# In the heavy experts of a mixture-of-experts block, the four gate tiles of a slice are computed before its four up tiles

## The reference, cut to what matters

```
def moe_swiglu(h, w_router, w_gate, w_up, w_down):
    logits = jnp.einsum('bsd,de->bse', h, w_router).astype(jnp.float32)
    top_v, top_i = lax.top_k(logits, TOP_K)
    wts = jax.nn.softmax(top_v, axis=-1)
    gates = jnp.sum(jax.nn.one_hot(top_i, N_EXPERTS, dtype=jnp.float32) * wts[..., None], axis=-2)

    def per_seq(args):
        hb, gb = args
        a = jnp.einsum('sd,edf->sef', hb, w_gate)
        u = jnp.einsum('sd,edf->sef', hb, w_up)
        act = jax.nn.silu(a) * u * gb[:, :, None]
        return jnp.einsum('sef,efd->sd', act, w_down)
```

## Time and profile before

| | us |
|---|---|
| median of three launches | 2583.78 |
| the three launches | 2572.14, 2583.78, 2585.42 |
| the profiled launch, its own time | 2578.32 |
| its span, from the first to the last instruction | 2576.3 |
| TensorE busy in the span | 2470.6 (96%) |
| VectorE, ScalarE busy | 652.9, 375.5 |
| experts, from the first heavy rise to the last residual matmul | 703.4 to 1698.6 |

### The profile page before, as it was taken

The page is one execution under the profiler, slowest core; times in us unless marked ns, Lnnn a source line. Parts: engine busy times, 40 slices in busy tenths (PEclk is TensorE's granted clock), DMA queues, the critical chain, the costliest instruction groups (busy, mean ns, idle before and its releaser), DMA issues.

```text
span 2576.3 us, 34065 instructions
## 1 busy us (share of the span) xinstructions
PE 2470.6 (96%) x14632; PEld 1945.3 (76%) x14633; DVE 652.9 (25%) x1854; ACT 375.5 (15%) x973; POOL 28.0 (1%) x52
## 2 busy tenths in 40 slices
PE   7999999998999989998999899989899999989999
PEld 4768888876888558855885687567578888658888
DVE  3663452167200001000000000024531112443111
ACT  3231000223200000000000000014420001441001
POOL 1010000001000000000000000000000000000000
PEclk9999999997999999999999999999999999999999
DMA  9381777422277999799979988992334442423420
GB/s 359 130 293 67 288 267 261 143 99 99 99 261 294 368 394 339 277 395 394 349 278 394 394 336 298 394 308 95 131 107 155 153 139 69 145 100 131 154 75 17
DMA packets 270058, 582.85 MB, mean 226 GB/s; under 512 B 19386, under 2 KB 46530, under 8 KB 269908
## 3 DMA queue, kind: packets, MB, share of 16 engines
q1 hardware_dynamic: 268900, 579.51, 61.5%
q10 hardware_dynamic: 432, 1.01, 0.1%
q0 software_dynamic: 576, 0.13, 0.0%
HBM read 579.58 MB, written 1.05 MB: 225 GB/s over the span
## 4 chain that ended last, share of the span: by engine, by line
PE 87%; DMA 6%; DVE 3%; ACT 2%; issue 1%; SPq 0%; DVEq 0%; ACTq 0%
PE wrk L2204 16%; PE acc L1582 12%; PE acc L835 9%; PE wrk L2890 9%; PE acc L2240 7%; PE wrk L1565 6%; PE wrk L2217 5%; DMA ring<-in_moe_w_up_dram 5%; PE acc L838 3%; PE acc L909 2%; PE acc L2251 2%; PE acc L924 2%; PE acc L739 1%; PE acc L2259 1%; PE acc L2267 1%; PE wrk L974 1%
## 5 line engine op out<-in xcount | busy, mean ns | idle before, releaser
L2204 PEld LDWEIGHTS wrk<-hT,ring 128*128 128x128 f32 x3584 | 408.5, 194 | 26.1 <-issue 14.9
L2204 PE MATMUL wrk<-hT,ring 128*128 128x128 f32 x3584 | 411.3, 277 | 16.0 <-DMA ring<-in_moe_w_up_dram 9.3
L1582 PE MATMUL acc<-scratch,ring 128*128 128x256 f32 x1376 | 300.4, 379 | 0.0
L1582 PEld LDWEIGHTS acc<-scratch,ring 128*128 128x128 f32 x1376 | 261.1, 190 | 35.3
L835 PE MATMUL acc<-hT,ring 128*128 128x256 f32 (+2 forms) x1152 | 262.9, 385 | 0.5 <-ACT scratch L865 0.5
L835 PEld LDWEIGHTS acc<-hT,ring 128*128 128x128 f32 (+2 forms) x1152 | 211.2, 186 | 41.1 <-issue 2.6
L2890 PE MATMUL wrk<-hT,ring 128*128 128x256 f32 x1024 | 223.3, 379 | 0.0
L2890 PEld LDWEIGHTS wrk<-hT,ring 128*128 128x128 f32 x1024 | 194.6, 190 | 26.5
L2217 PE MATMUL wrk<-ring,hT 128*64 128x256 f32 x1792 | 200.4, 381 | 4.6 <-DMA ring<-in_moe_w_up_dram 3.1
L2240 PE MATMUL acc<-ring,scratch 128*128 128x512 f32 x448 | 196.5, 593 | 0.0
L2217 PEld LDWEIGHTS wrk<-ring,hT 128*64 128x64 f32 x1792 | 126.3, 137 | 73.0 <-issue 8.1
(11 more groups left out here) (390 smaller groups left out, 2045.0 us busy)
## 6 DMA issues: line engine op xcount, KB each, us to landing
ring<-in_moe_w_gate_dram SPq DMA_DIRECT2D x56, 2048.0 KB, 13.5
ring<-in_moe_w_up_dram SPq DMA_DIRECT2D x56, 2048.0 KB, 11.6
ring<-in_moe_w_down_dram SPq DMA_DIRECT2D x56, 2048.0 KB, 14.2
ring<-in_w_ada_dram SPq DMA_DIRECT2D x24, 2048.0 KB, 15.0
ring<-in_w_up_dram SPq DMA_DIRECT2D x16, 2048.0 KB, 8.6
ring<-in_w_down_dram SPq DMA_DIRECT2D x16, 2048.0 KB, 7.6
ring<-in_w_out_dram SPq DMA_DIRECT2D x8, 2048.0 KB, 8.8
ring<-in_w_in_dram SPq DMA_DIRECT2D x8, 1536.0 KB, 12.6
```

What stands on the lines that cost most here:

```text
L1582: mm = pe.matmul(accv[:, m, :], w[:, j, m * P:(m + 1) * P], F_ACT[:, 4 * (g % 2) + j, :], start=(g == 0 and j == 0 and m % 2 == 0), stop=( ...
L2204: mm = pe.matmul(wrk[:, j, lo:lo + P], w[:, k, j * P:(j + 1) * P], hT[:, k, 0:P], start=(k == 0), stop=(k == KD - 1))
```

## The change: gate products first, then up products

The loops in `rise` are turned round: the outer loop goes over gate and up, the inner one over the four tiles. The gate's slot in the ring is therefore released after the fourth of eight products. A new semaphore `heavy_gate` tells ScalarE of the gate tiles 0 to 2, and `freed_by_pe` of gate tile 3, so that ScalarE makes the silu without the up product. Up tile j, which goes into the same PSUM bank, waits until the silu of gate tile j has been read out (`ffn_silu`). VectorE now waits for both the silu and the up product. ScalarE's copy of the next expert's tokens into `hT` waits for all up products of the expert before, which the silu's wait covered until now. The light experts and the order of the loads are as they were.

```
             def rise(e, g):
-                for j in range(4):
-                    pe.wait_ge(ffn_act, tile_of(e, 4 * g + j) - 3)
-                    for item, lo in ((("egate", g), 0), (("eup", g), S)):
-                        if j == 0:
-                            arrive(e, item)
-                        w = w_cols(item, 512)
+                for item, lo in ((("egate", g), 0), (("eup", g), S)):
+                    arrive(e, item)
+                    w = w_cols(item, 512)
+                    for j in range(4):
+                        if lo == 0:
+                            pe.wait_ge(ffn_act, tile_of(e, 4 * g + j) - 3)
+                        else:
+                            pe.wait_ge(ffn_silu, tile_of(e, 4 * g + j) + 1)
                         for k in range(KD):
                             mm = pe.matmul(wrk[:, j, lo:lo + P], w[:, k, j * P:(j + 1) * P], hT[:, k, 0:P],
                                            start=(k == 0), stop=(k == KD - 1))
-                        if lo == 0 and j == 3:
+                        if lo:
+                            mm.then_inc(ffn_up, 1)
+                        elif j == 3:
                             mm.then_inc(freed_by_pe, 1)
-                    mm.then_inc(ffn_up, 1)
+                        else:
+                            mm.then_inc(heavy_gate, 1)
...
             def tokens(e):
                 act.wait_ge(gathered, e + 1)
+                if e:
+                    act.wait_ge(ffn_up, tile_of(e, 0))
...
-                    act.wait_ge(ffn_up, tile_of(e, i + 1))
+                    g, j = i // 4, i % 4
+                    if j == 3:
+                        act.wait_ge(freed_by_pe, e * FREED + freeing(("egate", g)))
+                    else:
+                        act.wait_ge(heavy_gate, 3 * light_slice(e, g) + j + 1)
                     act.wait_ge(ffn_act, tile_of(e, i - 3))
                     act.activation(F_SIL[:, i % 4, 0:P], wrk[:, i % 4, 0:P], ACT.Silu).then_inc(ffn_silu, 1)
...
                     dve.wait_ge(ffn_silu, tile_of(e, i + 1))
+                    dve.wait_ge(ffn_up, tile_of(e, i + 1))
                     dve.tensor_tensor(F_ACT[:, 4 * (g % 2) + j, 0:P], F_SIL[:, j, 0:P], wrk[:, j, S:S + P], ALU.mult).then_inc(ffn_act, 1)
```

More of the change, by code:

```diff
@@ L294, in program @@
         light_turned, light_ready = sem("light_turned"), sem("light_ready")
+        heavy_gate = sem("heavy_gate")
         last_rows, last_weights, last_share = sem("last_rows"), sem("last_weights"), sem("last_share")
```

## The result

The changed kernel takes 2563.63 us (median of nine launches, 2556.92 to 2569.32), the kernel before 2577.99 us (median of nine, 2572.14 to 2586.52). The ratio is 0.9947, with a 95% interval of 0.9927 to 0.9966: faster by 0.5%, by 14.4 us. In a second measurement of both kernels the ratio was 0.9927 (0.9903 to 0.9951), 19 us between the medians.

A forecast was written before the change was run, and what follows sets the result against it. Heavy experts were taken as bound by TensorE, light experts by the weight transfers. The gain of 15.5 - 1.5 + 1.2 = 15.2 us, from a mean of 2579.9 us, gave 2564.7, rounded to 2565 us, range 2556 to 2574.

The forecast's parts named there:

- Gate products ahead of the wait: First rises of heavy experts 2, 4 and 6: four gate products cover the wait for up 0; 15.5 us gained.
- rival 2: First rises: the wait moves to gate 1 or up 1 instead of going; gain 1.2 us, 2579; chance 0.05.
- The clock: First rises: 4.4 of the 15.5 us need the clock to stay up; 1.5 us taken as still lost.
- Rival 1: Starts of heavy experts: the clock still falls at each, as in expert 2; gain 8.0 us, 2572; chance 0.08.
- The release in mid rise: Four passages from heavy to light: the gate's slot comes free 5.4 us sooner; 0.3 us gained each, 1.2 us together.
- the bound of 0.44: End of heavy expert 0: the third load behind starts at 855.57 instead of 856.01, so at most 0.44 us gained.
- Rival 3: Four passages from heavy to light: the mid-rise release is worth its full 5.4 us each; gain 37 us, 2543; chance 0.03.
- the releases named: End of heavy expert 0: the releases at 848.85 (down 5) and 855.57 (down 6), said not to move.
- Added waits and signals: All 28 rises: 84 more waits and 84 more signals, taken to cost 0; upper bound for the waits 27.7 us.
- Rival 4: The 84 added waits stop weight loads running ahead, 0.33 us each; 27.7 us less 15.2, slower at 2592; chance 0.05.
- The sum: Whole kernel: 15.5 - 1.5 + 1.2 = 15.2 us gained, adding up along the path; chance of the forecast 0.79.

The follow-up runs named there:

- all but three rises: The changed kernel with the old order in the first rise of heavy experts 2, 4 and 6 alone; 2581.95 us, ratio to before 1.0011.
- the moved addition: The changed kernel, with the results of light experts 1, 3 and 5 added in two experts later; 2545.45 us, ratio to before 0.9876.
- late release: The changed kernel with the gate's slot released at the seventh of a rise's eight products; 2564.63 us, ratio to before 0.9937.
- two ahead: The kernel before, with two gate products ahead in the first rise of heavy experts 2, 4 and 6; 2571.33 us, ratio 0.9974.
- filled wait: The kernel before, with 14 unused matmuls behind the first gate product of heavy experts 2, 4 and 6; 2575.54 us, ratio 0.9989.

## Why the prediction was right

*Gate products ahead of the wait: 15.5 us forecast, 15.2 measured* (58.56 - 43.38). The three experiments that vary nothing but this show it from three sides: alone it brings the gain (2564.35 us), without it nothing is gained (2581.95), and half of it shortens the rises as worked out (16.29 us against 16.1). The rise took 14.46 us where I had taken 14.35 from a row in mid expert. The 0.11 us more go with the addition behind it: in the version with the additions moved away the first two rises take 28.66 us together, 14.33 each. Nothing became late behind it, as worked out from the landing times: there is no wait for gate 1 or up 1, which was rival 2.

*The clock: 1.5 us forecast to stay lost, 0 measured.* That step erred in size and was on the safe side. Its reason was wrong in part as well. The prediction expected the clock loss to go because the longest idle piece, the wait for up 0, goes. But the largest loss, 2.9 of the 4.4 us in expert 2, belongs to a fall of the clock that came before this wait, inside the first gate product. That this part came back too doesn't follow from the prediction's argument; here it may have been lucky. With the old order the first rises cost 20.94, 19.58, 18.04, 19.51, 20.71 and 19.63 us in two profiles, a loss of 1.7 us on average over 18.04, near the 1.5 us (4.4 / 3) that the one profile showed. With four products ahead it was 0 in twelve of twelve. What decides it was not settled. Rival 1 is out for these profiles.

*The release in mid rise: 0.3 us a passage forecast, 0.4 measured.* Light experts 1, 3 and 5 take 88.85 us on average with the early release (12 values in four profiles: the changed kernel, its repetition, all but three rises, the moved addition) and 89.24 us with the release at the seventh product (12 values in four: before, late release, two ahead, filled wait). 0.39 us lies under the bound of 0.44. Eleven of the first twelve values lie between 88.59 and 88.97 us and all of the others between 89.03 and 89.42; one value with the early release, 89.43 us, falls out of its group. Rival 3, which would have made it 5.4 us, fails by exactly the releases named: they are the ones that TensorE's falls set. For a release at the rise's very end I forecast 2.2 us a passage against the early one and measured 1.8. About 0.2 us of the difference is the signal's place on the last matmul but one: the load went out at 846.22, which is 840.9 in the changed kernel's time (its expert 0 starts 5.33 us earlier), where 841.1 had been expected. The rest stays open.

*Added waits and signals: 0 forecast, 0 measured.* The rest of the four heavy experts takes 577.66 us before and after, to 0.01 us. It holds 25 of the 28 rises, and with them 75 of the 84 added waits and 75 of the 84 added signals. The chain of the changed kernel has the rises in mid expert at their old length:

```profile
784.41 14.35 PE wrk L2207 x128
...
805.63 14.29 PE wrk L2207 x128
```

Rival 4 does not show: a wait that has long been met, and one more signal on a matmul in a dense stream, are free here. Nor does the Trainium skill's price for signals of packed tiles show at this place (TensorE: Matmul & The Clock Gate, "The cost: per-tile semaphore tail"), which came to an estimate of 2.2 us for all 84 of them.

*The sum.* 15.2 + 1.2 = 16.4 us in the experts, against 15.2 forecast. The spans differ by 15.1 us, since the rest of the program took 1.3 us back (-0.7 and +2.0 in the table), and the medians by 14.4 us. The nine launches of either kernel spread over 12 to 14 us, and the interval of the ratio allows a gain of 9 to 19 us; the table by stretches settles where the gain lies. That the sum came out 0.8 us from the medians is closer than these allow one to claim.

## What to carry to other kernels

When a stream of weights is behind, look for work that needs only the load that has landed and do all of it before the first wait for the next one; what it takes off the wait can be worked out product by product. An earlier release of a buffer is worth only what lies between it and the next release in the same queue, so compare the whole row of releases, not the one that moves. And where two regimes take turns, one bound by the engine and one by the stream, work moved from the first into the second is the larger prize: here 10 to 12 us in the experts for nothing but another place in the program.

## What the runs showed of the hardware that was not expected

With one 2 MB load at a time in the queue, the DMA engines stand nearly still between two loads. The load issued at 848.12 in the changed kernel moves its data from about 849.1 to 855.3, 6.2 us (share 0.04 in the stretch from 848, 1.05 in that from 854 on), and at the four issues shown the stop lasts 0.4 to 1.0 us. With the queue never empty the same loads follow each other without a gap in 5.32 us.

The granted clock after the same waits differed from launch to launch and even between the three like places of one launch: 18.04, 19.58 and 20.94 us for the same rise. A single profile therefore prices this at 0 to 2.9 us a place, and no better. And the place of the fall differed too. In heavy expert 2 of the kernel before, the clock fell in a busy piece (945 to 947) with no idle piece over 1.86 us in the light expert ahead of it, while in expert 6 of the same launch it stayed up through an idle piece of 3.32 us.
